# Second attention: logits as three rounded products of 64 rows, both heads side by side, with queries and keys split by whole tiles a segment sooner

## The reference

```
q = rms_norm(q, q_norm_g);  k = rms_norm(k, k_norm_g)         # per head, 64 features
z = einsum(q, k) * 64**-0.5                                   # logits, causal: s < t
log_beta = log_sigmoid(z);  log_rem = log_sigmoid(-z)         # log_rem is 0 where not causal
weights  = exp(log_beta + suffix_sum(log_rem))                # 0 where not causal
o = einsum(weights, v)
```

## Time and profile before

| | |
|---|---|
| median of 3 runs | 2695.1 us (2694.73 to 2696.29) |
| span of the profiled execution, from first to last instruction | 2692.7 us |
| what the median has beyond that span | 2.4 us |
| busy share of the span: PE, PEld, DVE, ACT, POOL | 98, 80, 73, 42, 50% |
| chain that ended last: PE, DVE, ACT | 90, 5, 2% |
| the four pairs begin (first logits) at | 1513.82, 1579.50, 1647.20, 1714.86 us |

### The profile page before, as it was taken

How to read it: one execution, slowest core, us unless ns; L and a number is a source line. 1 busy time by engine, 2 the same in 40 slices (tenths; PEclk the granted TensorE clock), 3 DMA queues, 4 the chain that set the end, 5 groups by cost and what they waited for, 6 DMA issues and landing times.

```text
span 2692.7 us, 38261 instructions
## 1 busy us (share of the span) xinstructions
PE 2650.6 (98%) x14670; PEld 2141.7 (80%) x14670; DVE 1968.4 (73%) x2324; ACT 1120.6 (42%) x1628; POOL 1359.8 (50%) x878
## 2 busy tenths in 40 slices
PE   8999999999999999999999999999999999999999
PEld 6888877877788888888888766678778888888887
DVE  8777676778767766687778688855776566777775
ACT  5555533342433333344454355532243334444451
POOL 3111100002377777788945322132477777888842
PEclk9999999999999999999999999999999999999999
DMA  3111111113123323454412111112133445554512
GB/s 127 36 44 34 35 47 40 40 32 103 44 82 111 109 83 114 132 184 149 161 47 102 49 40 40 41 39 85 66 104 138 164 143 188 190 153 149 152 59 78
DMA packets 103439, 251.33 MB, mean 93 GB/s; under 512 B 10873, under 2 KB 14817, under 8 KB 99809
## 3 DMA queue, kind: packets, MB, share of 16 engines
q1 hardware_dynamic: 98944, 234.88, 27.0%
q10 hardware_dynamic: 4320, 14.09, 1.3%
HBM read 188.46 MB, written 58.11 MB: 92 GB/s over the span
## 4 chain that ended last, share of the span: by engine, by line
PE 90%; DVE 5%; ACT 2%; issue 1%; POOL 1%; DMA 0%; SPq 0%; ACTq 0%; DVEq 0%; POOLq 0%
PE ps L1210 10%; PE ps L1212 9%; PE ps L1211 9%; PE ps L1345 8%; PE ps L1347 8%; PE ps L1346 8%; PE ps L1395 6%; PE ps L1394 6%; PE ps L1393 6%; PE ps L1530 2%; PE ps L1759 1%; PE ps L1783 1%; PE ps L1769 1%; PE ps L1518 1%; PE ps L1504 1%
## 5 line engine op out<-in xcount | busy, mean ns | idle before, releaser
L1020 POOL TENSOR_TENSOR w_hi<-w_raw,der 128x1024 fp32r<-128x1024 f32 (+1 forms) x55 | 100.0, 1819 | 837.6 <-PE ps L1212 756.6
L1210 PE MATMUL ps<-a_hi,w_hi 128*128 128x512 f32 x1120 | 463.1, 413 | 11.3 <-POOL w_lo L1025 10.2
L1212 PE MATMUL ps<-a_hi,w_lo 128*128 128x512 f32 x1120 | 439.3, 392 | 0.0
L1211 PE MATMUL ps<-a_lo,w_hi 128*128 128x512 f32 x1120 | 438.1, 391 | 0.0
L1078 POOL TENSOR_TENSOR w_lo<-w_raw,w_hi 128x512 fp32r<-128x512 f32 x212 | 290.2, 1371 | 119.8 <-ACT w_hi L2845 119.6
L2845 ACT ACTIVATE w_hi<-w_raw 128x512 fp32r<-128x512 f32 (+1 forms) x249 | 169.3, 681 | 358.2 <-PE ps L1347 187.7
L2472 DVE TENSOR_TENSOR x<-ps,x 128x512 f32<-128x512 f32 x356 | 236.0, 688 | 31.5 <-PE ps L1395 31.5
L1210 PEld LDWEIGHTS ps<-a_hi,w_hi 128*128 128x128 f32 x1120 | 211.6, 189 | 57.0 <-issue 17.0
L1078 POOL TENSOR_TENSOR w_lo<-asum,w_hi 128x512 fp32r<-128x512 f32 x151 | 209.9, 1390 | 87.1 <-ACT w_hi L2845 87.1
L1212 PEld LDWEIGHTS ps<-a_hi,w_lo 128*128 128x128 f32 x1120 | 210.6, 188 | 46.4
L1211 PEld LDWEIGHTS ps<-a_lo,w_hi 128*128 128x128 f32 x1120 | 211.8, 189 | 35.2 <-issue 0.2
(11 more groups left out here) (473 smaller groups left out, 6693.7 us busy)
## 6 DMA issues: line engine op xcount, KB each, us to landing
fb_wait<-hidden SPq DMA_DIRECT2D x56, 512.0 KB, 3.8
w_raw<-in_w_mix SPq DMA_DIRECT2D x54, 512.0 KB, 3.5
hidden<-hcomb SPq DMA_DIRECT2D x27, 1024.0 KB, 3.9
w_raw<-in_w_f SPq DMA_DIRECT2D x96, 256.0 KB, 3.1
w_raw<-in_w_gu SPq DMA_DIRECT2D x88, 256.0 KB, 2.6
fa_wait<-hidden SPq DMA_DIRECT2D x28, 512.0 KB, 3.9
hidden<-hbuf SPq DMA_DIRECT2D x27, 512.0 KB, 5.6
w_raw<-in_w_ple SPq DMA_DIRECT2D x16, 512.0 KB, 3.5
```

The lines of the kernel that those rows point to most:

```text
L1210: mm(ps[:, bank, :], wh, hi[:, k, cols], start=(n == 0), stop=False)
L1211: mm(ps[:, bank, :], wh, lo[:, k, cols], start=False, stop=False)
L1212: last = mm(ps[:, bank, :], wl, hi[:, k, cols], start=False, stop=(n == nk - 1))
```

## The change

A tile `skh` holds the high part of the scaled queries and keys (4 KB each per partition, one for all pairs), and two tiles `skl` lie over `sk` itself: VectorE subtracts the high part from `sk` in place, so that what was `sk` becomes the low part. ScalarE makes the high part by a copy (`rounded_qk`, two instructions of 128 x 1024, once the scaling is done and the last pair's logits have been read), VectorE the low part (`remainders`, two instructions of 128 x 1024). `logits` issues three products for each head, the heads in turn within each product, and raises z_mm on the third. For pairs 1 to 3 the scaling moves from n = NSEG - 1 to n = NSEG - 2 on VectorE, the subtractions stand at NSEG - 1 and the copies at the end of iteration NSEG - 1 on ScalarE. For pair 0 the copies and subtractions stand ahead of the loop, and slot 0 of the projections moves ahead of the first logits on TensorE. TensorE's waits on qk2_ready become waits on qk_low.

```diff
         sk = [at("sk_even", (2, T), S0), at("sk_odd", (2, T), 128 * KB)]
+        skh = at("sk_high", (2, T), 152 * KB, F32R)
+        skl = [at("sk_low_even", (2, T), S0, F32R), at("sk_low_odd", (2, T), 128 * KB, F32R)]
...
                 s = NSEG * p + n
-                for hh in range(2):
-                    if s >= 2:
-                        pe.wait_ge(sa_done, 2 * (s - 2) + hh + 1)
-                    r = slice(64 * hh, 64 * hh + 64)
-                    mm(ps[:, 2 + 2 * (s % 2) + hh, 0:w], sk[p % 2][r, 0, j * P:(j + 1) * P],
-                       sk[p % 2][r, 1, k0:k0 + w], start=True, stop=True).then_inc(z_mm, 1)
+                lows = skl[p % 2]
+                for i, (qs, ks) in enumerate(((skh, skh), (skh, lows), (lows, skh))):
+                    for hh in range(2):
+                        if s >= 2 and i == 0:
+                            pe.wait_ge(sa_done, 2 * (s - 2) + hh + 1)
+                        r = slice(64 * hh, 64 * hh + 64)
+                        last = mm(ps[:, 2 + 2 * (s % 2) + hh, 0:w], qs[r, 0, j * P:(j + 1) * P],
+                                  ks[r, 1, k0:k0 + w], start=i == 0, stop=i == 2)
+                        if i == 2:
+                            last.then_inc(z_mm, 1)
...
             gemm_half(U_SB + 2, 1, U_SB % 2, a_hi, a_lo, KT, first=6)
-            pe.wait_ge(qk2_ready, 2)
+            norm_fill(0, sb_slots(0)[0])
+            pe.wait_ge(qk_low, 2 * HEADS + 2)
             logits(0, 0)
             logits(0, 1)
...
                         transposes(sv, 6, sv_tr)
-                        if p == 0:
-                            norm_fill(p, slots[0])
                         norm_fill(p, slots[1])
...
                         if n == NSEG and hh and more:
-                            pe.wait_ge(qk2_ready, 2 * p + 4)
+                            pe.wait_ge(qk_low, 2 * HEADS + 2 * p + 4)
                             logits(p + 1, 0)
                             logits(p + 1, 1)
...
             leave_half(U_SB + 2, 1, sv[:, :])
+
+            def remainders(p, t):
+
+                dve.wait_ge(qk_high, 4 * HEADS + 2 * p + t + 1)
+                tt(skl[p % 2][:, t, :], sk[p % 2][:, t, :], skh[:, t, :].bitcast(F32),
+                   ALU.subtract).then_inc(qk_low, 1)
+
+            for t in range(2):
+                remainders(0, t)
...
                     if p + 1 < HEADS and n == NSEG - 1:
+                        for t in range(2):
+                            remainders(p + 1, t)
+                    if p + 1 < HEADS and n == NSEG - 2:
                         dve.wait_ge(qk_fac_in, 64 * (p + 1))
...
+            def rounded_qk(p, t):
+
+                act.wait_ge(qk2_ready, 2 * p + t + 1)
+                if p:
+                    act.wait_ge(z_mm, 2 * NSEG * p)
+                av(skh[:, t, :], sk[p % 2][:, t, :], ACT.Copy).then_inc(qk_high, 1)
+
...
                     act.wait_ge(x_out, 16 * KT)
+                    rounded_qk(0, 0)
+                    rounded_qk(0, 1)
...
                     if p + 1 < HEADS:
+                        if n == NSEG - 1:
+                            rounded_qk(p + 1, 0)
+                            rounded_qk(p + 1, 1)
```

## The result

The changed kernel takes 2703.76 us (median of eight, 2701.95 to 2706.55), the kernel before 2695.86: a ratio of 1.0031 (95% interval 1.0022 to 1.0039), 7.9 us slower. The forecast was 2701.4 (+6.3 on the 2695.1 of then) and, as a rival, 2703.4 (+8.3) if TensorE's clock falls in the stall at the start. The interval, 5.9 to 10.5 us, holds both, so the time alone does not decide between them. The trace does: the clock fell.

A forecast was written before the change was run, and what follows sets the result against it. TensorE was taken as the bound, VectorE close behind. Start 3.5 + 0.04, borders 3 x 1.31 = 3.93, last pair 1.17 off: +6.3 us on 2695.1, giving 2701.4 us; range 2696.7 to 2705.5.

The forecast's parts named there:

- The logits: Steps of three rounded products, heads beside each other: 0.16 us less at 512 columns, 0.11 at 384, 0.05 at 256, 0.06 more at 128.
- The opening: A pair's first logits steps, 128 and 256 columns: 0.86 us start to start becomes about 0.90, 0.04 more.
- one step that saves nothing: In each of the first three pairs, one 512-column step only lengthens TensorE's 0.91 us idle time for a ScalarE copy.
- the last pair: Fourth head pair of the second attention: its full 1.17 us comes off, since no border follows.
- The start: First pair: subtractions alternate with GpSimd's splits, logits start at 1519.5 after a 4.7 us stall; 3.5 us later net.
- The clock: TensorE's clock in the start stall: no fall within the work taken, nothing added, 2701.4 us kept.
- the rival's +8.3: Clock falls in the start stall, some ten products take 0.2 us longer: +2.0, 2703.4 us; chance 0.18.
- at the lower level: Program's first stretch, where a product lasts 0.63 us, not 0.39; used to price the clock's fall.
- The borders: Three borders between pairs: subtractions add 2.28 us, less 1.01, plus 0.04, net 1.31 us each, 3.93 together.
- the two waits that the forecast named: At each border TensorE idles for a turn, then for qk_low, together 1.2 to 1.4 us more per pair.
- in a chain without a gap the order changes nothing in its length: VectorE at each border: moving the scalings ahead of segment 11's scans costs nothing; only two subtractions of 1.14 us add.
- The sum: Whole kernel: 3.5 + 0.04 at the start, 3.93 at the borders, 1.17 off in the last pair: +6.3 us.

The follow-up runs named there:

- GpSimd held back: Against the changed kernel, GpSimd's split of the third projection unit waits until both subtractions of the first pair are done; 2700.76 us, 1.0018 of before.
- the idle time filled: Changed kernel plus 16 more rounded products of 512 columns between slot 0 and the first pair's wait for the low parts; 2701.86 us, 1.0023 of before.
- border pieces: Changed kernel with border subtractions cut: first 256 columns where they stood, the other 768 a segment later, ahead of an eviction; 2701.49 us, 1.0022 of before.
- scaling back: Changed kernel with border scalings back behind segment 11's weights, copies and subtractions behind them; 2709.38 us, 1.0050 of before.

## Why the prediction was right, and where not

**The logits: right.** Forecast 0.90, 0.74, 0.58, 0.48 by width; measured 0.89, 0.73, 0.55 and 0.48. The opening was forecast at 0.90 from start to start and takes 0.88 (its logits at 1589.87, the next product at 1590.75); on the chain it takes 0.96 where it took 0.93. A pair with the moved scaling and the products but no subtractions is 67.98 us, with the moved scaling alone 69.05: 1.07 saved, where the steps' 1.17 less the opening's 0.04 makes 1.13 and the forecast, with one step that saves nothing, had 0.97. That step is there: the wait for ScalarE's copy grew from 0.91 to 1.08 us (in front of the turn at 1638.77). Only the last pair gave less, 0.7 to 0.8 us for 1.17. TensorE has one idle time of 0.26 us in it that before has not; the rest is open.

**The start: right but for the clock.** Forecast: split, subtraction, split, subtraction, 3.5 us later. Measured with the clock kept: 11.95 - 8.52 = 3.4, a stall of 4.33 us for 4.7. GpSimd held back shows the cause. The Trainium skill ("SBUF — State Buffer", section "Who interferes with whom") has it that VectorE shares its second port pair with GpSimd under an exclusive lock, and that a VectorE instruction with two inputs in SBUF contends with a GpSimd instruction that reads SBUF; 2.35 us without and 4.87 with the split agree.

**The clock: the step that failed.** The prediction took nothing for it and argued that the one fall in the trace of before came only after 4.3 us of idle time; it gave the fall a chance of 0.18 and a price of 2.0 us. By its own numbers that spoke for the fall, since its stall was 4.7 us long. Both profiles of the kernel show it, at 1.5 and 3.0 us, so do the three other profiles with a wait of 4.3 us or more at this place, and with the idle time filled it is gone. The measured +7.9 lies nearer to the rival's +8.3 than to the forecast's +6.3. The rival's price came from a row that it called "at the lower level". The granted clock of before reads 1.00 there, so the level was inferred; the products at 0.50 in the profile after have the same 0.63 us. The rule of the Trainium skill that the prediction weighed ("TensorE: Matmul & The Clock Gate", section "Loop structure matters more than you think"), that a long wait lets the clock drop, was right here, and the borders with one wait of 2.62 us agree with it too. The wait of 1.95 us near 40 us, followed by half clock in five of 13 profiles, shows that the length of a wait does not settle it alone.

**The borders: the sum right, its parts wrong.** Forecast +1.31 per border, measured +1.19, +1.17 and +1.20, by the two waits that the forecast named. But "in a chain without a gap the order changes nothing in its length; the subtractions add 2.28" prices one chain only. Before, two nearly equal ones met at the opening: VectorE's (weights, scalings) and TensorE's (turn, slot 24, turn), 0.26 us apart. With the scalings ahead, TensorE's stands behind VectorE's, which alone costs 1.39 us; the subtractions then run beside the turns and add 0.88, not 2.28. The sum of 2.27 came out right since the chain's last link comes 2.28 us later by either count. Whoever had used the parts, to cut the subtractions say, would have expected 2.28 us a border where 0.88 come back, as the run without them did.

**The sum, in part by luck.** The account with the idle time filled comes within 0.1 us of the forecast's +6.3, but two misses cancel in it: the three borders cost 3.6 us and not 3.9, and the last pair gives back 0.8 and not 1.2.

## What to carry to other kernels

When an instruction is moved forward on a gapless engine, ask what of the bounding engine's work stands behind each link: the chain keeps its length, but the work that lay beside its last links can come to lie behind them. Cut helper work by what the next consumer reads first; here 256 of 1024 columns first, with one split of GpSimd held back, turned a loss of 0.3% into a gain of 0.1%. A stall of TensorE can have a second price behind it, at half clock: here it followed all five waits of 4.3 us or more at the start and all three of 2.62 us at the borders, and none of the pairs of 1.42 and 0.81 us. So two short waits can be cheaper than one.

## What was not expected of the hardware

The half clock can begin after the wait is over: behind the wait of 2.62 us the logits start at 1585.83 and the stretch at 0.50 begins at 1587.70, 1.9 us later, so the price falls on the work that follows. In four profiles of the same stall of 4.33 to 4.35 us it lasted 6.8 us (the kernel after), 3.4 (its second profile), 3.4 (border pieces) and 3.4 (scaling back); what decides that was not tried, nor why the same 1.95 us near 40 us bring it in some executions only. In the measured times filling the idle time won 1.9 to 2.8 us (2701.86 against 2703.76 and 2704.66; against before of the same run 5.8 us more, where the kernel after takes 7.9 and 9.3).
